# Causal mask of an attention phase: added by VectorE in the score bank in place of a TensorE product with the unit matrix

## The reference, cut to what matters

```python
def mla_attention(q_nope, q_rope, k_nope, k_rope, v):
    scale = (QK_NOPE_DIM + QK_ROPE_DIM) ** -0.5
    ...
        scores = (jnp.einsum('bqhd,bkhd->bhqk', qn_b, k_nope)
                  + jnp.einsum('bqhd,bkd->bhqk', qr_b, k_rope)).astype(jnp.float32) * scale
        q_idx = i * Q_BLOCK + jnp.arange(Q_BLOCK)
        mask = key_idx[None, :] <= q_idx[:, None]
        scores = jnp.where(mask[None, None], scores, -jnp.inf)
        p = jax.nn.softmax(scores, axis=-1).astype(v.dtype)
        return jnp.einsum('bhqk,bkhd->bqhd', p, v)
```

## Time and profile before

| | us |
|---|---|
| median of 3 runs (2643.92 to 2645.95) | 2643.93 |
| the profiled execution: time | 2644.77 |
| its span, first to last instruction | 2642.7 |

### The profile page before, as it was taken

The page is one execution under the profiler, slowest core; times in us unless marked ns, Lnnn a source line. Parts: engine busy times, 40 slices in busy tenths (PEclk is TensorE's granted clock), DMA queues, the critical chain, the costliest instruction groups (busy, mean ns, idle before and its releaser), DMA issues. The chain is left out here.

```text
span 2642.7 us, 32568 instructions
## 1 busy us (share of the span) xinstructions
PE 2566.5 (97%) x12186; PEld 2114.8 (80%) x12186; DVE 1751.3 (66%) x2069; ACT 853.6 (32%) x1691; POOL 647.1 (24%) x585
## 2 busy tenths in 40 slices
PE   4999999999999999999999999999999999999998
PEld 4787888888888888788787887887887788888887
DVE  5677887989889899576467767767767621223342
ACT  3532111211111111243355565555555521111221
POOL 2223111111111111232043143133133320323422
PEclk8999999999999999999999999999999999999999
DMA  8033211312113121379712213112112164667532
GB/s 305 25 96 120 89 56 57 89 48 89 56 57 89 48 89 49 104 259 337 242 52 104 70 55 109 57 68 101 63 69 80 64 216 158 212 212 226 190 136 80
DMA packets 194240, 305.69 MB, mean 116 GB/s; under 512 B 18169, under 2 KB 111421, under 8 KB 184412
## 3 DMA queue, kind: packets, MB, share of 16 engines
q1 hardware_dynamic: 184412, 279.12, 32.1%
q0 software_dynamic: 5120, 16.78, 1.9%
q10 hardware_dynamic: 4608, 8.39, 0.9%
HBM read 200.97 MB, written 103.28 MB: 115 GB/s over the span
## 5 line engine op out<-in xcount | busy, mean ns | idle before, releaser
L52 PE MATMUL ps_proj<-h_hi,w_hi 128*128 128x512 f32 x1696 | 667.1, 393 | 9.1 <-DVE h_lo L807 6.8
L54 PE MATMUL ps_proj<-h_hi,w_lo 128*128 128x512 f32 x1696 | 660.7, 390 | 0.0
L53 PE MATMUL ps_proj<-h_lo,w_hi 128*128 128x512 f32 x1696 | 660.5, 389 | 0.0
L916 DVE SCALAR_TENSOR_TENSOR acc<-u,taps_t,acc 128x2048 f32<-128x2048 f32 x240 | 628.9, 2620 | 8.5
L52 PEld LDWEIGHTS ps_proj<-h_hi,w_hi 128*128 128x128 f32 x1696 | 318.7, 188 | 77.0 <-issue 7.5
L708 POOL TENSOR_TENSOR w_lo<-raw,w_hi 128x1024 fp32r<-128x1024 f32 x53 | 178.7, 3372 | 822.4 <-ACT w_hi L496 822.4
L53 PEld LDWEIGHTS ps_proj<-h_lo,w_hi 128*128 128x128 f32 x1696 | 318.8, 188 | 67.0 <-issue 1.9
L54 PEld LDWEIGHTS ps_proj<-h_hi,w_lo 128*128 128x128 f32 x1696 | 318.7, 188 | 66.4
L1765 POOL TENSOR_SCALAR prob<-prob,rinv 128x512 f32<-128x512 f32 (+2 forms) x320 | 200.3, 644 | 348.2 <-DVE rinv L1713 348.1
L1718 DVE TENSOR_TENSOR pt_lo<-ps_t,pt_hi 128x512 fp32r<-128x512 f32 (+1 forms) x320 | 194.2, 609 | 93.8 <-ACT pt_hi L1637 90.0
L1637 ACT ACTIVATE pt_hi<-ps_t 128x512 fp32r<-128x512 f32 (+1 forms) x320 | 169.7, 532 | 233.4 <-PE ps_t L1530 233.2
(11 more groups left out here) (227 smaller groups left out, 4027.7 us busy)
## 6 DMA issues: line engine op xcount, KB each, us to landing
qlat<-qlat_dram SPq DMA_DIRECT2D x32, 1024.0 KB, 5.8
raw<-in_w_in_dram SPq DMA_DIRECT2D x52, 512.0 KB, 6.4
under_h<-in_w_ada_dram SPq DMA_DIRECT2D x8, 1024.0 KB, 11.0
ga_dram<-lat SPq DMA_DIRECT2D x8, 1024.0 KB, 5.0
gb_dram<-lat SPq DMA_DIRECT2D x8, 1024.0 KB, 5.2
agate_dram<-lat SPq DMA_DIRECT2D x8, 1024.0 KB, 5.0
conv_dram<-acc SPq DMA_DIRECT2D x8, 1024.0 KB, 3.9
v_dram<-v_st SPq DMA_DIRECT2D x4, 2048.0 KB, 8.5
```

What stands on the lines that cost most here:

```text
L52: pe.matmul(out, wh, xh, start=first, stop=False)
L53: pe.matmul(out, wh, xl, start=False, stop=False)
L54: return pe.matmul(out, wl, xh, start=False, stop=last)
L916: dve.scalar_tensor_tensor(acc[:], u[:, n:n + S], tap(n), acc[:], ALU.mult, ALU.add).then_inc(conv_tap if n < TAPS - 1 else conv_done, 1)
```

## The change

The sixth product of the diagonal chunk goes; its semaphore count moves to the fifth. Before the maximum of a diagonal chunk VectorE adds the mask to the 128x128 square in the same bank, signals a new semaphore and waits for it.

```diff
@@ attention_phase, TensorE @@
-                        mm = pe.matmul(out, qr[:, q], k.kr_lo2[:, ks], start=False, stop=(c < g))
-                        if c == g:
-
-                            mm = pe.matmul(out[:, b * P:(b + 1) * P], k.ident16[:], k.mask[:], start=False, stop=True)
-                        mm.then_inc(scores_mm, 1)
+                        pe.matmul(out, qr[:, q], k.kr_lo2[:, ks], start=False, stop=True).then_inc(scores_mm, 1)
@@ attention_phase, VectorE @@
                                 dve.wait_ge(scores_mm, at.scores(chunk_no[n, c] + 1))
+                                if c == g:
+                                    own = ps[:, chunk_no[n, c] % RING, b * P:(b + 1) * P]
+                                    dve.tensor_tensor(own, own, k.mask[:], ALU.add).then_inc(masked, 1)
+                                    dve.wait_ge(masked, at.block(n + 1))
                                 ins = dve.tensor_reduce(to, ps[:, chunk_no[n, c] % RING, 0:width], AX.X, ALU.max,
                                                         negate=True)
```

More of the change, by code:

```diff
@@ L1306, in attention_phase @@
         scores_mm = sem("scores_mm")
+        masked = sem("masked")
         max_step = sem("max_step")
```

## The result

The changed kernel takes 2677.85 us (median of 4 runs, 2676.35 to 2678.14), the kernel before 2643.93. The ratio is 1.0124, with a 95% interval of 1.0112 to 1.0136: slower by 33.9 us, where +10 was forecast, and outside the stated range. The profiled execution took 2677.62 us, its span is 2675.5, 32.8 more than before.

What follows compares the result with a forecast made beforehand. TensorE, 97% busy, was taken to be held at each head's start by the chain through VectorE's maximum and ScalarE's exp. Six heads at +1.5, last +0.5, first +0.6 gave +10.1 us: 2654.5 us, range 2640 to 2664.

Steps and rivals of the forecast that it cites:

- the sum: All eight heads: six at +1.5 us, the last +0.5, the first +0.6, together +10.1 us; nothing outside attention changes.
- the walk: Block-by-block account of one head, each place with its change in when TensorE goes on: +1.5 us a head.
- blocks 0 to 4, restart of TensorE: Head's start, VectorE the limit: four additions of 0.325 us delay exp and TensorE's restart, +1.30 us.
- block 6: No slack between maximum and exp, so the addition's delay reaches TensorE: +0.24 us.
- blocks 7 to 9: TensorE waits for a tile copy, then GpSimd's scaling; saved products are worth almost nothing: -0.04 us.
- block 11: Addition delays the tile's low part, using up the slack and the saved product's gain: +0.08 us.
- blocks 12 and 13: No tile follows tightly, so both saved products count: -0.25 us together.
- block 15, to the next head: The tile already waits 0.18 us for VectorE's low part, so the addition's delay counts: +0.25 us.
- The product's slot: Time each removed mask product takes on TensorE: 0.125 us, 16.0 us if all 128 were on its path.
- The first rival: TensorE is the limit everywhere, all 128 slots are won: 2628 us, chance 0.12.
- The second: Head's start loses as forecast, but tile stretches of blocks 10, 11, 14, 15 keep their slots: 2646 to 2649, chance 0.2.
- The third: VectorE becomes the limit at every block, additions putting 41.6 us on the path: 2685.5 us, chance 0.06.

Runs made afterwards that it cites:

- e3: Kernel before with 32 idle semaphore increments in VectorE's loop body, no arithmetic more: 2658.53 us, ratio 1.0051.
- e9: Changed kernel, loop and all additions kept, their semaphore cleared each turn so waits are against constants (body of 255 instructions): 2656.77 us, ratio 1.0045.
- e12: Kernel before with 20 idle semaphore increments in VectorE's loop body, 258 instructions: 2645.82 us against 2645.52, one run.
- e1: Changed kernel with VectorE's loop over the first 7 heads written out as straight code: 2657.11 us, ratio 1.0043.
- e2: Kernel before with only VectorE's loop written out as straight code, mask still by TensorE: 2645.84 us, ratio 0.9999.
- e4: Kernel before with the mask left out altogether, neither product nor addition, so not a usable version: 2640.04 us, ratio 0.998.
- e7: Changed kernel, VectorE's loop written out, VectorE adding only in blocks 0 to 4, TensorE's product in the rest: 2654.29 us against 2643.53, one run.
- e8: Changed kernel, VectorE's loop written out, VectorE adding only in blocks 5 to 15, TensorE's product in the rest: 2650.36 us against 2643.53, one run.
- e5: Kernel before with 16 idle semaphore increments in VectorE's loop body, 254 instructions: 2650.54 us against 2643.53, one run.
- e6: Kernel before with 24 idle semaphore increments in VectorE's loop body, 262 instructions: 2662.81 us against 2643.53, one run.

## Why the prediction was wrong

**The step that failed** is the sentence that closes the sum: nothing outside the attention phase changes, no DMA is moved, no queue is passed. I counted the additions as time on VectorE, and not as length of its program; the register step of each wait I did not count at all. The runs show in its place 32 more instructions in VectorE's loop body, five more packets on the instruction queue in each turn, and 21 to 23 us. No rival held this mechanism either. The rows that would have raised the question were at hand: before, the instruction queue is silent through the loop, 2 packets in 630 us, which says that the bodies stay in memory. That the limit was near, some 260 instructions against 238, no row of before shows. The Trainium skill, "Runtime: NRT & Kernel Launch" (Instruction fetch mechanics), says that a taken branch whose target is not in the window of two pages forces a DMA fetch before execution goes on; e3 shows such a stall, and e9 and e12, with shorter bodies, have none. The same section of the Trainium skill gives 256 instructions to a block and two blocks to the window. By estimate from these figures a body of 270 would pass, unless it begins so near the end of a block that it reaches into a third one; a step between 258 and 262 would mean a start with two to five instructions of its block left. The runs fit that but do not show it, since none moved the start of the loop.

**The rest of the walk was right in its mechanism,** and e1 against e2 measures it place by place. VectorE in the third head of e2 (loop written out, mask by TensorE):

```profile
1515.84 1.75 DVE L1683 TENSOR_TENSOR qr<-rope_a,qr 64x512 fp32r<-64x512 f32 x1
1517.62 0.62 DVE L1695 TENSOR_REDUCE nbias<-ps_ring 128x1 f32<-128x128 f32 x2
1519.80 0.16 DVE L1713 RECIPROCAL rinv<-rsum 128x1 f32<-128x1 f32 x1 [1.55 <-ACT prob L1629]
...
1523.34 0.16 DVE L1701 TENSOR_REDUCE nbias<-nmax 128x1 f32<-128x4 f32 x1
```

and in e1 (loop written out, mask by VectorE):

```profile
1517.08 1.75 DVE L1680 TENSOR_TENSOR qr<-rope_a,qr 64x512 fp32r<-64x512 f32 x1
1518.75 0.28 DVE L1694 TENSOR_TENSOR ps_ring<-ps_ring,mask 128x128 f32<-128x128 f32 x1
1519.07 0.29 DVE L1696 TENSOR_REDUCE nbias<-ps_ring 128x1 f32<-128x128 f32 x1
...
1521.24 0.16 DVE L1714 RECIPROCAL rinv<-rsum 128x1 f32<-128x1 f32 x1 [1.22 <-ACT prob L1626]
1521.32 0.28 DVE L1694 TENSOR_TENSOR ps_ring<-ps_ring,mask 128x128 f32<-128x128 f32 x1
1521.64 0.56 DVE L1696 TENSOR_REDUCE nbias<-ps_ring 128x1 f32<-128x384 f32 x1
...
1525.60 0.16 DVE L1702 TENSOR_REDUCE nbias<-nmax 128x1 f32<-128x4 f32 x1
```

Counted from the rope step (L1683, there L1680), the last row comes at 7.50 us in e2 and at 8.52 in e1: +1.02 where the walk has +1.30. From one step to the next an addition and its wait are 1521.64 - 1521.32 = 0.32 us, as forecast at 0.325. The first one is cheaper: it starts at 1518.75, before the rope step's end at 1518.83, where the maximum had to wait until 0.03 after it, so only 1.99 - 1.78 = 0.21 are left. The three that follow the reciprocal stretch the way to the last row from 3.54 to 4.36 us, 0.27 each. The other places, as TensorE's last score product of each block in the two timelines moves against the head's start:

| place | forecast | e1 less e2 |
|---|---|---|
| blocks 0 to 4, restart of TensorE | +1.30 | +1.03 |
| block 5 | 0 | +0.01 |
| block 6 | +0.24 | +0.29 |
| blocks 7 to 9 | -0.04 | 0.00 |
| block 10 | 0 | -0.02 |
| block 11 | +0.08 | +0.03 |
| blocks 12 and 13 | -0.25 | -0.17 |
| block 14 | -0.05 | -0.04 |
| block 15, to the next head | +0.25 | +0.20 |
| a head | +1.5 | +1.36 (by heads) |

- The product's slot, 0.125 us by the earlier trace rows, was too dear: in blocks 12 and 13, where TensorE is the limit, two of them are worth 0.17, so 0.085 each, and e4 gives 0.7 us a head for what I put at 1.0. The place does not explain it: in block 12 another score chunk follows, as in the earlier trace rows, and from L1515 (in e1 L1516) of the one to the same product of the other take 1568.68 - 1567.52 = 1.16 us in e2 and 1571.22 - 1570.14 = 1.08 in e1. What was wrong is the reading of the slot as the difference of two starts, 0.35 - 0.23.
- The first rival, TensorE the limit everywhere, is out by e4. The second, gains and losses cancel, needed 0.4 to 0.75 a head and met 1.36. The third, VectorE's backlog never caught up, asked for 41.6 us from the additions, which gave 11.3, and for an even spread in e7 and e8. Its 2685.5 us came nearer to the measured time than my sum did, by chance.
- The whole addition gives +11.3 us (e1 less e2) or +11.25 (e9 less its before), where the sum has +10.1. That the two are near is in part luck. From e2 to e1 the six turns grow by 8.0 us (9.0 forecast), the first head by 0.25 (0.6) and the last by 2.8 (0.5), and the last one's clock is 0.96 in e1 and 0.98 in e2.

**Where the 33.9 us are.** 11.3 is the addition. The refetch in a kernel without additions is 13 (e3). The two together make 24.4; the changed kernel has 9 more. Three steps of VectorE divide the profiled execution, the rope step ahead of the second head, the one ahead of the last, and its last step with the gate. Before:

```profile
1413.68 1.74 DVE L1683 TENSOR_TENSOR qr<-rope_a,qr 64x512 fp32r<-64x512 f32 x1
2019.66 1.75 DVE L1683 TENSOR_TENSOR qr<-rope_a,qr 64x512 fp32r<-64x512 f32 x1
2112.68 0.69 DVE L1726 TENSOR_TENSOR bg<-ps_o,bg 128x512 f32<-128x512 f32 x1 [0.64 <-PE ps_o L1547]
```

and after:

```profile
1415.69 1.75 DVE L1680 TENSOR_TENSOR qr<-rope_a,qr 64x512 fp32r<-64x512 f32 x1
2048.56 1.75 DVE L1680 TENSOR_TENSOR qr<-rope_a,qr 64x512 fp32r<-64x512 f32 x1
2145.63 0.69 DVE L1727 TENSOR_TENSOR bg<-ps_o,bg 128x512 f32<-128x512 f32 x1 [0.64 <-PE ps_o L1544]
```

So of the 32.8 us of the span 2.0 are there before the second head, 26.9 lie in the six turns (632.87 us against 605.98) and 4.0 in the last head (97.07 against 93.02). The same six turns grow by 8.0 from e2 to e1 and by 13.9 from the kernel before to e3, 21.9 together. Only 5.0 of the 9 us that remain are in the turns, then, the part of the loop. The windows over the starts of four of these heads show the clock (length, busy us of the engines with counts, PEclk, DMA, GB/s):

```profile
1519.00:1534.00 15.00, 11.42 (x48) 8.83 (x48) 9.46 (x23) 6.52 (x16) 3.41 (x5) 0.89 0.69 237
1624.00:1639.00 15.00, 10.69 (x54) 8.18 (x53) 9.85 (x23) 7.08 (x17) 3.42 (x5) 1.00 0.67 237
1730.00:1745.00 15.00, 11.92 (x44) 9.39 (x45) 9.07 (x22) 6.50 (x18) 3.42 (x5) 0.77 0.67 238
1836.00:1851.00 15.00, 12.12 (x45) 9.56 (x46) 9.11 (x22) 6.73 (x19) 3.41 (x5) 0.77 0.68 238
```

The granted clock of a stretch is a mean over its two levels, 2.4 and 1.2 GHz; at 0.77 nearly half of the 15 us was at 1.2. With the waits of TensorE at 5 us in the start of a head, its clock falls in some heads and not in others. The head that begins at 1628.92, at full clock, takes 104.92 us; the one at 1523.54, with 0.89, 105.38; the ones at 1733.84 and 1839.95, with 0.77, 106.11 and 105.73. So full-clock heads have about 101.0 + 1.3 + 2.5, and the clock adds 0.5 to 1.2 on top in the heads where it falls. In e1 and e9 it does not fall in any head of the loop. The six turns are 19.1 us longer than in e1, of which six times the 2.5 of the full-clock heads are 15; by this estimate some 4 of the 5.0 us are the clock's and 1 is a stall that costs more than in e3. There it ends ahead of the reciprocal, for which VectorE waits 1.55 us even without it (e2); in the changed kernel the addition and the maximum of block 1 still stand between, 1422.37 - 1421.69 = 0.68 us. No run held the clock up with the rest unchanged, so these shares are read and not shown.

The 2.0 us ahead of the second head and the 4.0 in the last one are not the refetch's: e9, without a refetch, has them too, its second head's rope step at 1416.26 and a last head of 97.10 us. The first of them stand already at the first head's table load, 1315.68 against 1313.66, which has only one addition ahead of it; in e5, whose edit lies behind that point, it comes at 1317.68. The last head has the additions in it, but its clock varies from one kernel to the next as well:

```profile
2035.61:2126.51 90.90, 84.82 (x477) 69.53 (x476) 60.23 (x133) 53.17 (x132) 36.00 (x45) 1.00 0.22 70
2048.56:2145.63 97.07, 89.30 (x462) 73.87 (x461) 63.98 (x149) 53.29 (x132) 36.00 (x45) 0.93 0.21 66
```

The first row is the last head of e3, with TensorE's mask product and at full clock, the second that of the changed kernel. What the additions cost there, apart from the clock, stays open.

## What to carry to other kernels

An instruction put into a loop body has a length as well as a duration. Ask whether the body still stays in the engine's program memory, look whether the instruction queue is silent in the loop, and count the register steps that waits against loop-dependent values bring along. Where a wait is against a constant, it needs no register step: e9 took 15 instructions out of the body in that way. And an engine that is 97% busy can still be idle at the few places where a second engine's chain decides; price a step there by the chain, not by the slot it frees.

## What the runs showed of the hardware

- A loop body of VectorE with up to 258 instructions (238, 248, 254, 255, 256 and 258 were run) had no refetch, one of 262 or 270 had five packets of 8 KB in every turn behind the first, all with the same start of the loop. The cost was 1.8 to 3.5 us a turn in e3 and e6, the upper end with a clock of 0.98. Written out as straight code, the same work ran without a stall; the queue moved 38 packets in the whole of e1 against 30 in the kernel before.
- 20 semaphore increments in VectorE's loop body, where it mostly idles, left the heads at 101.0 us (e12).
- VectorE's addition in place in PSUM, float32 with a bf16 operand from SBUF, 128x128: 0.279 to 0.300 us, like the one that writes SBUF; a dependent step starts 0.03 us behind it.
